# Expert token rows split once into two rounded parts, the gate moved to the scatter, six raw unit buffers

## Chip, cores and metric

One core of one Trainium2 chip runs the whole program. The metric is the device time in microseconds of one execution. A product is rounded when its operands are float32r, plain when they are float32.

## What is computed

The reference is one inference step of a two-layer decoder over 256 new tokens and 8 x 8 sampled ones, 320 tokens of width 1024. Each layer has a token mixer and a feed-forward part; in layer 0 it is dense, in layer 1 a mixture of eight experts, of which each token takes its best two:

```python
logits = x @ w_router + b_router
top_val, top_idx = lax.top_k(logits, 2)
gate = einsum(softmax(top_val), one_hot(top_idx, 8))
for e in range(8):
    out = out + gate[..., e:e + 1] * ((silu(x @ w_gate[e]) * (x @ w_up[e])) @ w_down[e])
```

with w_gate and w_up of 1024 x 2816 and w_down of 2816 x 1024 per expert. The layer's result is a layer norm of ALPHA * x + out. All of it is float32.

## The kernel before

Only the expert stage of layer 1 is touched. It works in this way.

**Tokens.** The normalised tokens x1T lie with their features on the partitions. tensor_moe (L1035) makes the router's logits on PE (L1041) and turns the tokens into rows (to_rows, L936); scalar_moe (L1370) copies these rows into xtk, three chunks of 128, 128 and 64 tokens with 1024 columns each (L1374). vector_moe (L1913) finds the chosen experts, the gates, and for each token its place in each expert's list, pos (L1970). xtk's unused 64 rows are set to zero (L1918). An expert has at most 128 places in one pass; further passes exist under a flag.

**Gather.** select(x) on DVE (L1827) makes a 0/1 matrix from pos, one column per place. gather(x) on PE (L941) multiplies the rows by it: 8 feature chunks times 3 token chunks, 24 plain products of 128 x 128 (L950). Then it turns the selection (L953), and with three products of one column makes the gate of each place (L955). ACT copies the result into a rounded tile (tokens_high, L1327) and the gate into gsl (L1329); DVE takes the difference (tokens_rest, L1842). From there on each product is three rounded ones, high x high, high x rest, rest x high (split_product, L561 to L565).

**Units.** An expert's weights come in 33 units of 1 MB. A unit is loaded by SP (unit_load, L2487, issued at L2498), copied by ACT into a rounded tile (expert_high, L1320), its difference is made by DVE (expert_rest, L1836), and PE multiplies with it: columns (L959) for gate and up, down (L979). There are MOE_RAW = 8 raw buffers: six in the tile weights and two in arena. Unit n waits, in SP's queue, until DVE has finished unit n - 8 (L2484). ACT and DVE run AHEAD = 3 units ahead of PE, over MOE_SPLIT = 4 rounded buffers. UNITS (L187) is the order in which all engines walk; tile by tile of 512 of the 2816 columns come gate units, up units and then the down units of the tile before. gather(x + 1) stands in PE's order inside expert x, behind its fourth tile (L1030).

**Gate and scatter.** gated(tile) on DVE (L1847) multiplies silu, gsl and the up product. After an expert's last down unit its output is split again (L1348, L1867), scatter on PE (L1002) multiplies it by the turned selection in six pieces of 512 columns, and add on DVE (L1870) adds each to acc, which began as ALPHA * xtk (L1883). PE's first gather waits for that scaling too (L947).

The first six units of the stage are loaded while the mixer of layer 1 still runs, each into a slot that the mixer has done with; units 6 and 7 go into arena as soon as the residual is made (L2576).

Of the kernel before, what the change touches and what calls it, by code (L numbers as in the profile page):

```python
# [6 lines left out]
P = 128  # L7
# [19 lines left out]
FF_SPLIT = 4  # L27
MOE_RAW = 8
MOE_SPLIT = 4
# [184 lines left out]
def build(nc, I, O, table):  # L214
    ctx = ExitStack()
    with ctx:
# [177 lines left out]

        xtk = view(a_kt, 3, D)
        acc = view(a_g, 3, D)

        raw = [view(i * UNIT, UNIT, of=weights) for i in FIRST_FREE] + [view(0, UNIT), view(a_o + 512, UNIT)]
        split_at = [a_u, a_u + UNIT, a_u + 2 * UNIT, a_v]
# [26 lines left out]
        gain = view(FIRST_FREE[0] * UNIT, D, of=weights)  # L426
        shift = view(FIRST_FREE[0] * UNIT + D, D, of=weights)
        selm = [room(3, P) for _ in range(2)]
        gsl = [room(1) for _ in range(2)]
        lg, expl, chosen, gate, pos = [room(3, NE) for _ in range(5)]  # L430
# [122 lines left out]
        def chunk(n):  # L553
            return slice(n * P, (n + 1) * P)
# [3 lines left out]
        def _(pe):  # L558
# [379 lines left out]

            def experts(ps):

                def gather(x):  # L941

                    pe.wait_ge(mo_sel, NE * ps + x + 1)
                    if x >= 2:
                        pe.wait_ge(mo_acc, NE * NP * ps + NP * (x - 1) + 1)
                    elif x == 0:
                        pe.wait_ge(mo_acc, NE * NP * ps + 1)  # L947
                    for k in range(KC):
                        for t in range(3):
                            nc.tensor.matmul(bank[5 + k // 4][:, chunk(k % 4)], xtk[:, t, chunk(k)],  # L950
                                             selm[x % 2][:, t, :], start=t == 0, stop=t == 2)
                    for t, (t0, r) in enumerate(TT):
                        nc.tensor.transpose(bank[7][:, t0:t0 + r], selm[x % 2][0:r, t, :], ident[0:r, 0:r])  # L953
                    for t in range(3):
                        mm = nc.tensor.matmul(bank[7][:, T:T + 1], selm[x % 2][:, t, :], gate[:, t, x:x + 1],  # L955
                                              start=t == 0, stop=t == 2)
                    mm.then_inc(mo_gath, 1)
# [77 lines left out]
            def tensor_moe(l):  # L1035
# [19 lines left out]
                pe.wait_ge(*dv_s.at("pos"))  # L1055
                pe.wait_ge(*ac_s.at("xtk"))
                experts(0)
                flag = pe.value_load(over, min_val=0, max_val=1)
# [116 lines left out]
        def _(act):  # L1175
# [146 lines left out]
            def experts(ps):  # L1322

                def tokens_high(x):
                    act.wait_ge(mo_gath, NE * ps + x + 1)
                    for i in range(2):
                        nc.scalar.activation(xgh[x % 2][:, 4 * i:4 * i + 4, :],  # L1327
                                             bank[5 + i].rearrange("p (k t) -> p k t", k=4), ACT.Copy).then_inc(mo_xh, 1)
                    nc.scalar.activation(gsl[x % 2], bank[7][:, T:T + 1], ACT.Copy)  # L1329
                    nc.scalar.activation(selT[x % 2], bank[7][:, 0:T], ACT.Copy).then_inc(mo_st, 1)  # L1330
# [39 lines left out]
            def scalar_moe(l):  # L1370
                for t, (t0, r) in enumerate(TT):
                    for i in range(2):
                        act.wait_ge(*pe_s.at("xt", l, t, i))
                        nc.scalar.activation(xtk[0:r, t, 512 * i:512 * i + 512], of(l, "xt", t, i)[0:r, :], ACT.Copy)\  # L1374
                            .then_inc(*free(ac_s, l, "xt", t, i))
                table[("act", "xtk")] = ac_s.count
                act.wait_ge(*dv_s.at("less max"))
                nc.scalar.activation(expl, expl, ACT.Exp).then_inc(*ac_s.done("exp logits"))
                act.wait_ge(*dv_s.at("pos"))
                for n, c in (("cp", 16 * HB), ("n", 32), ("conv", 32)):  # L1380
                    act.wait_ge(stored[n], c * (l + 1))
                for n in range(AHEAD):
                    expert_high(0, n)
                experts(0)
                flag = act.value_load(over, min_val=0, max_val=1)
                with act.If(flag > 0):
                    with act.Fori(1, 3) as ps:
                        for n in range(AHEAD):
                            expert_high(ps, n)
                        experts(ps)  # L1390
# [247 lines left out]
        def _(dve):  # L1638
# [186 lines left out]
            def experts(ps, first=False):  # L1825

                def select(x):  # L1827
                    if x >= 2:
                        dve.wait_ge(mo_gath, NE * ps + x - 1)
                    for t in range(3):  # L1830
                        ins = nc.vector.tensor_scalar(selm[x % 2][:, t, :], iotaF, pos[:, t, x:x + 1], None, ALU.is_equal)
                        ins.then_inc(*((mo_v, 1) if t < 2 else (mo_sel, 1)))
# [14 lines left out]
                def gated(tile):  # L1847
                    _, x, q, _, n = TILES[tile]
                    dve.wait_ge(mo_sil, NTILE * ps + tile + 1)
                    if q == 0:  # L1850
                        dve.wait_ge(mo_st, NE * ps + x + 1)
                    if tile > 0:
                        dve.wait_ge(mo_turn, NTILE * ps + tile)
                    nc.vector.scalar_tensor_tensor(hid[:, 0:n], sil[:, 0:n], gsl[x % 2], bank[1][:, 0:n], ALU.mult, ALU.mult)\
                        .then_inc(mo_h, 1)
# [14 lines left out]
                def add(x, c0, c1):  # L1870

                    dve.wait_ge(mo_acc, NE * NP * ps + NP * x + c0 + 1)
                    for p in range(c0, c1):
                        t, _, r, half = PIECES[p]
                        w = slice(512 * half, 512 * half + 512)
                        dve.wait_ge(mo_sc, NE * NP * ps + NP * x + p + 1)
                        nc.vector.tensor_tensor(acc[0:r, t, w], acc[0:r, t, w], bank[(7, 5, 6)[p % 3]][0:r, :], ALU.add)\
                            .then_inc(mo_acc, 1)

                select(0)  # L1880
                if first:
                    dve.wait_ge(*ac_s.at("xtk"))
                    nc.vector.tensor_scalar(acc, xtk, ALPHA, None, ALU.mult).then_inc(mo_acc, 1)  # L1883
                for n in range(AHEAD):
# [28 lines left out]
            def vector_moe(l):  # L1913
# [3 lines left out]
                nc.vector.memset(lg, 0.0).then_inc(*dv_s.done())  # L1917
                nc.vector.memset(xtk[NS:P, 2, :], 0.0).then_inc(*dv_s.done())  # L1918
                nc.vector.tensor_tensor(after_, causal, ident, ALU.subtract).then_inc(*dv_s.done())
# [523 lines left out]
        def _(sp):  # L2443
# [84 lines left out]
            for l in range(DEPTH):  # L2528
# [43 lines left out]
                else:  # L2572
                    for n in range(6):
                        sp.wait_ge(*pe_s.at("unit", l, *LAST_IN[FIRST_FREE[n]]))
                        unit_load(n)
                    sp.wait_ge(*dv_s.at("res1", l, KC - 1))  # L2576
                    unit_load(6)
                    unit_load(7)
                    experts(0, MOE_RAW)
# [59 lines left out]
```

## Time and profile before

| | us |
|---|---|
| median of three runs | 2387.61 (2387.57 to 2389.4) |
| the profiled execution, its own time | 2387.4 |
| its span, first to last instruction | 2385.5 |
| PE busy in the span | 2202.8 (92%) |
| DVE busy | 1578.8 (66%) |
| ACT busy | 1137.2 (48%) |
| POOL busy | 104.2 (4%) |

The span is what the trace covers; the execution's own time has 1.9 us around it. PE counts products, PEld weight loads, which overlap them; the end of a product is modelled, so the distance from one start to the next is what a product costs in a stream. A plain (f32) product leaves two loads and two products in the trace, a rounded one leaves one of each. The clock is the share of full speed granted to PE: 1.00 is 2.4 GHz, 0.50 is 1.2 GHz. Stretches named here are microseconds from the start of the span; the expert stage begins at about 1530.

### The profile page before, as it was taken

The page shows a single profiled execution, that of the slowest core. Times are in us where ns is not written, and L with a number is a line of the kernel's source. Part 1 is how long each engine was busy: PE and PEld are TensorE (multiplying, and loading weights), DVE is VectorE, ACT ScalarE, POOL GpSimd, SP SyncE. Part 2 cuts the span into 40 slices and gives each one's busy share as a digit, 9 for nine tenths or more (in the row PEclk, how much of TensorE's full clock was granted, in tenths as well). Part 3 has the DMA queues.
Part 4 walks back from the last instruction along what each step waited for, and adds up shares of the span by engine and source line. Part 5 has one row for each costly group of instructions (what it writes and reads, how often), then busy time and mean ns, then how long its engine had stood idle before and what let it go on. Part 6 is the DMA issues. An engine that isn't in the chain of part 4 may idle for free.

```text
span 2385.5 us, 31380 instructions
## 1 busy us (share of the span) xinstructions
PE 2202.8 (92%) x13148; PEld 1931.1 (81%) x13148; DVE 1578.8 (66%) x1787; ACT 1137.2 (48%) x1134; POOL 104.2 (4%) x173
## 2 busy tenths in 40 slices
PE   7889999899899988989998899799999999999996
PEld 6778767779799987878677799678888888888884
DVE  5746646656544435664745655488898988889896
ACT  4443333233333335353234232467676766767673
POOL 1001012000000000001021000000000000000000
PEclk9999999899899998999899999799999999999998
DMA  5232543654245432233525654399899999999992
GB/s 171 71 93 76 168 120 118 217 194 140 91 148 159 144 99 89 71 93 102 179 75 183 218 162 146 137 332 328 321 368 317 365 321 365 328 316 364 327 349 91
DMA packets 290491, 474.27 MB, mean 199 GB/s; under 512 B 17946, under 2 KB 160554, under 8 KB 290344
## 3 DMA queue, kind: packets, MB, share of 16 engines
q1 hardware_dynamic: 280652, 445.45, 55.3%
q0 software_dynamic: 9600, 26.75, 3.5%
q8 instruction: 106, 1.74, 0.3%
q14 instruction: 41, 0.34, 0.0%
q10 hardware_dynamic: 92, 0.00, 0.0%
HBM read 440.14 MB, written 29.92 MB: 197 GB/s over the span
## 4 chain that ended last, share of the span: by engine, by line
PE 49%; DVE 4%; ACT 2%; issue 1%; DMA 1%; SPq 0%; DVEq 0%; ACTq 0%
PE bank L563 10%; PE bank L565 10%; PE bank L564 10%; PE bank L569 3%; PE bank L571 3%; PE bank L570 3%; PE bank L950 2%; DVE mixer_rest L1682 1%; PE bank L999 1%; ACT mixer_high L1197 1%; PE bank L1014 0%; PE bank L1013 0%; PE bank L791 0%; PE bank L926 0%; PE bank L1041 0%
## 5 line engine op out<-in xcount | busy, mean ns | idle before, releaser
L1836 DVE TENSOR_TENSOR unit_rest<-weights,unit_high 128x2048 fp32r<-128x2048 f32 x198 | 452.0, 2289 | 85.8 <-ACT unit_high L1320 85.2
L1320 ACT ACTIVATE unit_high<-weights 128x2048 fp32r<-128x2048 f32 x198 | 379.3, 1919 | 158.9 <-PE bank L565 157.2
L1682 DVE TENSOR_TENSOR mixer_rest<-weights,mixer_high 128x2048 fp32r<-128x2048 f32 x86 | 196.5, 2287 | 231.1 <-ACT mixer_high L1197 231.0
L569 PE MATMUL bank<-tokens_in_high,mixer_high 128*128 128x320 f32 x896 | 295.3, 330 | 44.7 <-DVE mixer_rest L1682 37.7
L563 PE MATMUL bank<-unit_high,tokens_high 128*128 128x512 f32 (+1 forms) x768 | 291.2, 379 | 2.0 <-DVE tokens_rest L1842 2.0
L570 PE MATMUL bank<-tokens_in_rest,mixer_high 128*128 128x320 f32 x896 | 288.9, 322 | 0.0
L571 PE MATMUL bank<-tokens_in_high,mixer_rest 128*128 128x320 f32 x896 | 288.4, 322 | 0.0
L565 PE MATMUL bank<-unit_high,tokens_rest 128*128 128x512 f32 (+1 forms) x768 | 287.0, 374 | 0.0
L564 PE MATMUL bank<-unit_rest,tokens_high 128*128 128x512 f32 (+1 forms) x768 | 286.8, 373 | 0.0
L569 PEld LDWEIGHTS bank<-tokens_in_high,mixer_high 128*128 128x128 f32 x896 | 180.5, 201 | 52.1 <-DVE mixer_rest L1682 43.5
L1197 ACT ACTIVATE mixer_high<-weights 128x2048 fp32r<-128x2048 f32 x86 | 163.7, 1906 | 112.9 <-PE bank L571 58.2
L570 PEld LDWEIGHTS bank<-tokens_in_rest,mixer_high 128*128 128x128 f32 x896 | 179.7, 201 | 0.2
L571 PEld LDWEIGHTS bank<-tokens_in_high,mixer_rest 128*128 128x128 f32 x896 | 178.9, 200 | 0.0
L1836 DVE TENSOR_TENSOR unit_rest<-arena,unit_high 128x2048 fp32r<-128x2048 f32 x66 | 150.8, 2289 | 29.2 <-ACT unit_high L1320 28.9
L563 PEld LDWEIGHTS bank<-unit_high,tokens_high 128*128 128x128 f32 x768 | 145.5, 189 | 26.7 <-DVE tokens_rest L1842 2.1
L565 PEld LDWEIGHTS bank<-unit_high,tokens_rest 128*128 128x128 f32 x768 | 145.4, 189 | 26.0
L564 PEld LDWEIGHTS bank<-unit_rest,tokens_high 128*128 128x128 f32 x768 | 145.6, 190 | 24.5
L1320 ACT ACTIVATE unit_high<-arena 128x2048 fp32r<-128x2048 f32 x66 | 126.6, 1919 | 52.7 <-PE bank L565 52.7
L563 PE MATMUL bank<-unit_high,hidden_high 128*128 128x512 f32 x352 | 137.1, 390 | 1.1 <-DVE hidden_rest L1860 1.1
L565 PE MATMUL bank<-unit_high,hidden_rest 128*128 128x512 f32 x352 | 137.1, 390 | 0.0
L564 PE MATMUL bank<-unit_rest,hidden_high 128*128 128x512 f32 x352 | 137.0, 389 | 0.0
L1179 ACT ACTIVATE arena<-bank 128x320 f32<-128x320 f32 (+2 forms) x72 | 35.3, 490 | 212.6 <-PE bank L571 132.0
(417 smaller groups left out, 4317.7 us busy)
## 6 DMA issues: line engine op xcount, KB each, us to landing
weights<-in_w_ex_gate SPq DMA_DIRECT2D x67, 1024.0 KB, 6.7
weights<-in_w_in SPq DMA_DIRECT2D x66, 1024.0 KB, 5.3
weights<-in_w_ex_up SPq DMA_DIRECT2D x66, 1024.0 KB, 6.5
weights<-in_w_ex_down SPq DMA_DIRECT2D x65, 1024.0 KB, 6.8
arena<-in_w_ex_down SPq DMA_DIRECT2D x23, 1024.0 KB, 7.2
arena<-in_w_ex_up SPq DMA_DIRECT2D x22, 1024.0 KB, 7.1
arena<-in_w_ex_gate SPq DMA_DIRECT2D x21, 1024.0 KB, 7.0
weights<-in_state_mlstm_c SPq DMA_DIRECT2D x14, 1024.0 KB, 7.6
```

Source lines behind the costliest of these rows:

```text
L563: nc.tensor.matmul(out, xh, wh, start=start, stop=False)
L564: nc.tensor.matmul(out, xh, wl, start=False, stop=False)
L565: return nc.tensor.matmul(out, xl, wh, start=False, stop=stop)
L569: nc.tensor.matmul(out, wh, xh, start=start, stop=False)
L570: nc.tensor.matmul(out, wh, xl, start=False, stop=False)
L571: return nc.tensor.matmul(out, wl, xh, start=False, stop=stop)
L950: nc.tensor.matmul(bank[5 + k // 4][:, chunk(k % 4)], xtk[:, t, chunk(k)], selm[x % 2][:, t, :], start=t == 0, stop=t == 2)
L1179: nc.scalar.activation(dst, of(l, name, i, m)[0:rows, 0:cols], ACT.Copy)\
L1197: nc.scalar.activation(split_at_home(l, *u)[0], place_, ACT.Copy).then_inc(*ac_s.done("unit high", l, *u))
L1320: nc.scalar.activation(high[n % MOE_SPLIT], raw[n % MOE_RAW], ACT.Copy).then_inc(mo_high, 1)
L1682: nc.vector.tensor_tensor(wl, unit_at(l, *u)[0], wh, ALU.subtract).then_inc(*dv_s.done("unit rest", l, *u))
L1836: nc.vector.tensor_tensor(rest[n % MOE_SPLIT], raw[n % MOE_RAW], high[n % MOE_SPLIT], ALU.subtract)\
```

## The change

The token rows are no longer kept as they are and gathered by plain products. ACT copies the rows from PSUM into acc, then copies acc into a rounded tile xth; DVE subtracts xth from acc into three rounded tiles xtl, and only then scales acc by ALPHA. The selection is written as a rounded tile. gather multiplies first xth, then xtl, for each feature chunk and token chunk: 48 rounded products where 24 plain ones stood; the third chunk is used with its 64 rows alone, so nothing has to be set to zero. The first gather waits for xtl and no longer for the scaled acc.

The products that gathered the gate, ACT's copy of it and DVE's wait for that copy are gone. gated multiplies silu and up only; add multiplies each scattered piece by the token's gate while it adds it.

xtl takes the places of the two raw buffers in arena. So there are six, SP waits for unit n - 6, and the two loads behind the residual are gone.

```diff
@@ -25,7 +25,7 @@
 FF_SPLIT = 4
-MOE_RAW = 8
+MOE_RAW = 6
 MOE_SPLIT = 4
@@ -392,10 +392,11 @@
 
-        xtk = view(a_kt, 3, D)
+        xth = rounded("token_rows_high", a_kt, 3, D)
+        xtl = [rounded(f"token_rows_rest{t}", at, D) for t, at in enumerate((0, D, a_o + 512))]
         acc = view(a_g, 3, D)
 
-        raw = [view(i * UNIT, UNIT, of=weights) for i in FIRST_FREE] + [view(0, UNIT), view(a_o + 512, UNIT)]
+        raw = [view(i * UNIT, UNIT, of=weights) for i in FIRST_FREE]
         split_at = [a_u, a_u + UNIT, a_u + 2 * UNIT, a_v]
@@ -425,8 +426,9 @@
         shift = view(FIRST_FREE[0] * UNIT + D, D, of=weights)
+        room((-at[0]) % 8)
+        selr = [rounded(f"selection{i}", at[0] + 3 * P * i, 3, P) for i in range(2)]
         selm = [room(3, P) for _ in range(2)]
-        gsl = [room(1) for _ in range(2)]
         lg, expl, chosen, gate, pos = [room(3, NE) for _ in range(5)]
@@ -936,24 +938,23 @@
 
-            def experts(ps):
+            def experts(ps, first=False):
 
...
                         pe.wait_ge(mo_acc, NE * NP * ps + NP * (x - 1) + 1)
-                    elif x == 0:
+                    elif x == 0 and not first:
                         pe.wait_ge(mo_acc, NE * NP * ps + 1)
                     for k in range(KC):
-                        for t in range(3):
-                            nc.tensor.matmul(bank[5 + k // 4][:, chunk(k % 4)], xtk[:, t, chunk(k)],
-                                             selm[x % 2][:, t, :], start=t == 0, stop=t == 2)
+                        out = bank[5 + k // 4][:, chunk(k % 4)]
+                        for t, (_, r) in enumerate(TT):
+                            for i, rows in enumerate((xth[0:r, t, :], xtl[t][0:r, :])):
+                                nc.tensor.matmul(out, rows[:, chunk(k)], selr[x % 2][0:r, t, :],
+                                                 start=t + i == 0, stop=t + i == 3)
                     for t, (t0, r) in enumerate(TT):
-                        nc.tensor.transpose(bank[7][:, t0:t0 + r], selm[x % 2][0:r, t, :], ident[0:r, 0:r])
-                    for t in range(3):
-                        mm = nc.tensor.matmul(bank[7][:, T:T + 1], selm[x % 2][:, t, :], gate[:, t, x:x + 1],
-                                              start=t == 0, stop=t == 2)
+                        mm = nc.tensor.transpose(bank[7][:, t0:t0 + r], selm[x % 2][0:r, t, :], ident[0:r, 0:r])
                     mm.then_inc(mo_gath, 1)
@@ -1053,8 +1054,8 @@
                 pe.wait_ge(*dv_s.at("pos"))
-                pe.wait_ge(*ac_s.at("xtk"))
-                experts(0)
+                pe.wait_ge(*dv_s.at("xtl"))
+                experts(0, True)
                 flag = pe.value_load(over, min_val=0, max_val=1)
@@ -1326,7 +1327,6 @@
                                              bank[5 + i].rearrange("p (k t) -> p k t", k=4), ACT.Copy).then_inc(mo_xh, 1)
-                    nc.scalar.activation(gsl[x % 2], bank[7][:, T:T + 1], ACT.Copy)
                     nc.scalar.activation(selT[x % 2], bank[7][:, 0:T], ACT.Copy).then_inc(mo_st, 1)
@@ -1371,11 +1371,14 @@
                         act.wait_ge(*pe_s.at("xt", l, t, i))
-                        nc.scalar.activation(xtk[0:r, t, 512 * i:512 * i + 512], of(l, "xt", t, i)[0:r, :], ACT.Copy)\
+                        nc.scalar.activation(acc[0:r, t, 512 * i:512 * i + 512], of(l, "xt", t, i)[0:r, :], ACT.Copy)\
                             .then_inc(*free(ac_s, l, "xt", t, i))
...
                 nc.scalar.activation(expl, expl, ACT.Exp).then_inc(*ac_s.done("exp logits"))
+                act.wait_ge(*ac_s.at("xtk"))
+                nc.scalar.activation(xth[:, 0:2, :], acc[:, 0:2, :], ACT.Copy)
+                nc.scalar.activation(xth[0:NS, 2, :], acc[0:NS, 2, :], ACT.Copy).then_inc(*ac_s.done("xth"))
                 act.wait_ge(*dv_s.at("pos"))
@@ -1828,7 +1831,7 @@
                     for t in range(3):
-                        ins = nc.vector.tensor_scalar(selm[x % 2][:, t, :], iotaF, pos[:, t, x:x + 1], None, ALU.is_equal)
+                        ins = nc.vector.tensor_scalar(selr[x % 2][:, t, :], iotaF, pos[:, t, x:x + 1], None, ALU.is_equal)
                         ins.then_inc(*((mo_v, 1) if t < 2 else (mo_sel, 1)))
@@ -1847,11 +1850,9 @@
                     dve.wait_ge(mo_sil, NTILE * ps + tile + 1)
-                    if q == 0:
-                        dve.wait_ge(mo_st, NE * ps + x + 1)
                     if tile > 0:
                         dve.wait_ge(mo_turn, NTILE * ps + tile)
-                    nc.vector.scalar_tensor_tensor(hid[:, 0:n], sil[:, 0:n], gsl[x % 2], bank[1][:, 0:n], ALU.mult, ALU.mult)\
+                    nc.vector.tensor_tensor(hid[:, 0:n], sil[:, 0:n], bank[1][:, 0:n], ALU.mult)\
                         .then_inc(mo_h, 1)
@@ -1874,13 +1875,21 @@
                         dve.wait_ge(mo_sc, NE * NP * ps + NP * x + p + 1)
-                        nc.vector.tensor_tensor(acc[0:r, t, w], acc[0:r, t, w], bank[(7, 5, 6)[p % 3]][0:r, :], ALU.add)\
+                        nc.vector.scalar_tensor_tensor(acc[0:r, t, w], bank[(7, 5, 6)[p % 3]][0:r, :], gate[0:r, t, x:x + 1],
+                                                       acc[0:r, t, w], ALU.mult, ALU.add)\
                             .then_inc(mo_acc, 1)
...
                 if first:
-                    dve.wait_ge(*ac_s.at("xtk"))
-                    nc.vector.tensor_scalar(acc, xtk, ALPHA, None, ALU.mult).then_inc(mo_acc, 1)
+                    dve.wait_ge(*ac_s.at("xth"))
+                    for t, (_, r) in enumerate(TT):
+                        nc.vector.tensor_tensor(xtl[t][0:r, :], acc[0:r, t, :], xth[0:r, t, :], ALU.subtract)\
+                            .then_inc(*dv_s.done())
+                    table[("dve", "xtl")] = dv_s.count
+                    settle()
+                    nc.vector.tensor_scalar(acc[:, 0:2, :], acc[:, 0:2, :], ALPHA, None, ALU.mult).then_inc(*dv_s.done())
+                    nc.vector.tensor_scalar(acc[0:NS, 2, :], acc[0:NS, 2, :], ALPHA, None, ALU.mult).then_inc(mo_acc, 1)
+                    settle()
                 for n in range(AHEAD):
@@ -1915,7 +1924,6 @@
                 nc.vector.memset(lg, 0.0).then_inc(*dv_s.done())
-                nc.vector.memset(xtk[NS:P, 2, :], 0.0).then_inc(*dv_s.done())
                 nc.vector.tensor_tensor(after_, causal, ident, ALU.subtract).then_inc(*dv_s.done())
@@ -2573,9 +2581,6 @@
                         unit_load(n)
-                    sp.wait_ge(*dv_s.at("res1", l, KC - 1))
-                    unit_load(6)
-                    unit_load(7)
                     experts(0, MOE_RAW)
```

## Rows read from the trace of the kernel before

**Rows 1.** Page part 4: the chain that ended last, by engine

```profile
PE 49%; DVE 4%; ACT 2%; issue 1%; DMA 1%; SPq 0%; DVEq 0%; ACTq 0%
```

**Rows 2.** Busy us gather to gather: PE, PEld, DVE, ACT, POOL; clock, DMA share

```profile
1610.68:1712.92 102.24, 102.24 (x513) 86.17 (x512) 88.06 (x59) 70.71 (x52) 0.00 (x0) 1.00 0.95 341
...
sum 715.62, PE 715.62 PEld 603.11 DVE 616.12 ACT 494.90 POOL 0.00; mean PE 102.23 PEld 86.16 DVE 88.02 ACT 70.70 POOL 0.00
```

**Rows 3.** Timeline of PE at the second gather: start us, us, instruction

```profile
1610.68 5.52 PE L950 MATMUL bank<-arena 128*128 128x128 f32 x48
1616.04 0.58 PE L953 MATMUL bank<-arena 128*128 128x128 f32 x3
1616.56 0.83 PE L955 MATMUL bank<-arena 128*128 128x1 f32 x6
1617.25 0.48 PE L563 MATMUL bank<-unit_high,tokens_high 128*128 128x512 f32 x1
```

**Rows 4.** The chain that ended last, at the first gather: start, us, what

```profile
1527.88 0.23 ACT arena L1378
...
1529.71 0.68 DVE arena L1831 x3
1530.39 1.68 DVE arena L1883
...
1532.20 7.23 PE bank L950 x48
...
1540.65 0.61 ACT tokens_high L1327
...
1547.27 1.92 ACT unit_high L1320
```

**Rows 5.** Weight loads by form near 1615 and 1683: busy us, mean ns

```profile
L950 PEld LDWEIGHTS bank<-arena 128*128 128x128 f32 x48 | 5.4, 192 | 0.0
...
L1013 PEld LDWEIGHTS bank<-outputs_high,selection_turned 128*128 128x128 f32 x4 | 0.8, 188 | 0.2
...
L1013 PEld LDWEIGHTS bank<-outputs_high,selection_turned 128*64 128x64 f32 x2 | 0.3, 134 | 0.1
```

**Rows 6.** Timeline of PE in 256-wide rounded products

```profile
1636.85 0.28 PE L565 MATMUL bank<-unit_high,tokens_rest 128*128 128x256 f32 x1
...
1637.92 0.28 PE L565 MATMUL bank<-unit_high,tokens_rest 128*128 128x256 f32 x1
```

**Rows 7.** Groups of ACT and DVE with 1024 columns: busy us, mean ns

```profile
L1296 ACT ACTIVATE dense_high<-weights 128x1024 fp32r<-128x1024 f32 x2 | 2.1, 1062 | 10.3 <-PE bank L571 10.3
...
L1794 DVE TENSOR_TENSOR dense_rest<-weights,dense_high 128x1024 fp32r<-128x1024 f32 x2 | 2.5, 1226 | 6.2 <-ACT dense_high L1296 6.2
```

**Rows 8.** Busy us by stretch, columns as above, around the first gather

```profile
1512.10:1519.00 6.90, 6.90 (x33) 6.88 (x33) 1.42 (x4) 0.00 (x0) 0.00 (x0) 0.50 0.00 0
1528.90:1535.60 6.70, 3.40 (x16) 3.43 (x17) 6.60 (x13) 5.51 (x3) 0.00 (x0) 0.50 0.03 2
...
1559.60:1562.90 3.30, 3.30 (x9) 2.55 (x8) 1.35 (x2) 0.00 (x0) 0.00 (x0) 0.50 1.01 390
```

**Rows 9.** Waits of SP's queue from 1480 on: us in total, times, longest

```profile
SPq L2498 <- DVE unit_rest L1836: 733.6, 256, 38.1
```

**Rows 10.** Landings of all unit loads (L2498)

```profile
DMA to landing us min/median/max: 4.9/6.7/9.2
```

**Rows 11.** Timeline of SP and ACT for one unit and the load two on

```profile
1658.37 0.37 SPq L2498 DMA_DIRECT2D arena<-in_w_ex_up  x1
...
1663.81 0.37 SPq L2498 DMA_DIRECT2D weights<-in_w_ex_down  x1
...
1676.26 1.92 ACT L1320 ACTIVATE unit_high<-arena 128x2048 fp32r<-128x2048 f32 x1 [0.80 <-PE bank L565]
```

**Rows 12.** Groups of DVE by form, 1640 to 1720: busy us, mean ns

```profile
L1854 DVE SCALAR_TENSOR_TENSOR arena<-arena,bank 128x512 f32<-128x512 f32 x4 | 2.9, 737 | 0.0
...
L1877 DVE TENSOR_TENSOR arena<-arena,bank 128x512 f32<-128x512 f32 x4 | 2.5, 678 | 0.0
```

## Prediction

> **What bounds the kernel now.** I began at the page: PE holds 49% of the chain that ended last, all else that it names 8% together [rows 1]. The change touches only the expert stage, so I cut that stage into experts, from the start of one gather to the start of the next. All seven such stretches are alike: 102.2 us, PE busy in every one of them, DVE for 88 us, ACT for 71 us, the clock at 1.00 [rows 2]. Whatever PE no longer does there comes straight off the time, until another engine has no air: DVE has 14 us of it per expert. Then I read what PE does between two experts' units [rows 3]: the gather (24 f32 products, each recorded as two loads and two products, 48 records in 5.36 us from 1610.68 to 1616.04), three turns (0.52 us), and three products with the gate column (6 records, 0.69 us from 1616.56 to 1617.25). Last I read the chain at the first gather, the one place where PE waits on a string of other engines [rows 4].
>
> **The gate products go.** They end each gather, so 0.69 us of PE goes from seven stretches: 7 x 0.69 = **4.8 us less**. The first gather's share is in the sum of the start, below. ACT also loses its copy of the gate column; ACT has 31 us of air per expert, so that is worth nothing.
>
> **The gather, 24 f32 products against 48 rounded ones.** The name "single-pass" suggests half the work. But each of the 48 takes a fresh 128 x 128 weight load, and the old code has 48 loads as well. The gate products stream one column each and still took 0.69 / 6 = 115 ns, against 5.36 / 48 = 112 ns for a record that streams 128 columns twice [rows 3]. So at full clock the load sets the pace, not the stream. Is a rounded operand's load any shorter? No: 188 ns for the rounded 128 columns of L1013 and 134 for 64, beside 192 for the f32 ones of L950 [rows 5]; the difference of 54 ns per 64 columns makes about 107 ns of loading per 128. No rounded product as narrow as 128 columns is in the trace. From below: the 256-wide rounded products start 119 ns apart (nine steps from 1636.85 to 1637.92 [rows 6]), and if columns alone counted, 128 would take 59 ns, 2.9 us per gather. From above, as rounded products: those same 119 ns, 5.7 us. I take 112 ns, the row with the same load, the same width and the same neighbours: 48 x 112 ns = 5.4 us, **no change**; the two ends per gather are -2.5 and +0.35 us. The third chunk's products on 64 rows I cost as full ones.
>
> The Trainium skill ("TensorE: Matmul & The Clock Gate", Back-to-back issue gap) gives about 81 ns for a load and product pair of 128 columns, and its section on weight-path perf modes lets the fast weight load work for types other than FP32. By that the gather would be an estimated 3.9 us; the rows show the rounded load as long as the f32 one, which speaks against it.
>
> **The start of the expert stage.** Before: selection on DVE from 1529.71, then the scaling of all token rows until 1532.07, then PE [rows 4]. After: ACT, free at 1528.1, copies the rows into a rounded tile, 1.9 us for two chunks of 1024 columns (as the unit copy at 1547.27, 2048 columns [rows 4]) and 1.06 for the third [rows 7], until 1531.1. DVE, done with selecting at 1530.4, waits 0.7 us for it and makes three differences of 1024 columns, 1.2 us each [rows 7], until 1534.7. The scaling, now in two pieces of together some 1.8 us (L1883 took 1.7 [rows 4]), stands behind them and no longer ahead of the gather. So the gather starts at about 1534.85, **2.65 us later**. What stands behind the new work: ACT's first three unit copies start at 1531.1 and not 1529.71; DVE's first two unit differences end at 1534.7 + 1.9 + 4.5 = 1541.1. Both are hidden as long as the gather lasts to 1545; if it were 3.5 us long they would show.
>
> The clock there is at 0.50 from 1528.90 to 1535.60 [rows 8], since PE had nothing to do. In the old gather, two full streams per load followed and the clock came back after 16 records of 213 ns; the whole took 7.23 us [rows 4]. The logits' f32 products, which stream 8 columns behind each load, ran 6.9 us without a break, 209 ns each, and the clock stayed at 0.50 throughout [rows 8]: loads without much streaming did not bring it back. The new gather streams half of what the old one did per load, so I expect it at the lower level to its end: 48 x 213 ns = 10.2 us, three turns 0.6, and 0.25 to ACT: 1545.9, where ACT's copy began at 1540.65 [rows 4]: **5.25 us later**. The first unit's products then start in the slow clock too; 0.35 us more. Together **+5.6 us** (ends +2.6, if the clock comes back as before, and +6.5). The missing wait of the first gather for the scaled rows is in this sum.
>
> **Six raw buffers.** A load is issued when DVE has finished the unit that held the slot: all 256 waited for that, 734 us in total [rows 9], so the queue always stands ready. Loads land 9.2 us after issue at the latest, 6.7 in the middle [rows 10]. One unit in full: issued 1658.37, read by ACT at 1676.26, 17.9 us later. With six slots it goes out when the load two units on did, at 1663.81: 12.5 us before its reader [rows 11]. The longest landing leaves 3.3 us. **Zero**; if landings became 4 us longer, each further microsecond would be PE's per unit. At the start units 6 and 7 are no longer loaded ahead; they follow the first two differences (1538.9, 1541.1), land by 1550.3; ACT copied unit 4 at 1547.27 [rows 4], two units of 1.9 us before it could take unit 6, and all of that moves 5.6 us back. Hidden.
>
> **Vector forms.** The hidden rows lose a scalar operand (737 ns towards the 678 of a plain one), the scattered rows gain one (678 to about 737) [rows 12]: within 0.5 us per expert on DVE, hidden by its 14. Behind the last scatter two such adds are in the open: **+0.1**. The dropped memset ran while DVE waited for the logits: zero.
>
> **Sum.** -4.8 + 0 + 5.6 + 0 + 0.1 = +0.9 us on the profiled execution's 2387.4 (span 2385.5 and 1.9 around it): 2388.3; the median of the runs is 0.2 above that execution, so 2388.5. A measurement here can tell about 0.2%, 4.8 us, from no change: this forecast is no change.
>
> **Rivals.**
> 1. *The clock falls inside the later gathers* (slower). Place: the 5.4 us gather of each expert, where the stream per load is half of the old one. For it: the clock did sit at 0.50 through 6.9 us of load-bound products [rows 8]. Against it: that stretch streamed 8 columns, this one 128, and it comes straight out of dense products at 1.00. Price: a stretch at 0.50 (1.2 GHz) ran nine 512-wide products in 3.30 us [rows 8] where 2.4 GHz does it in half the time: 1.65 us lost per such stretch, twice that if the thin gather keeps it down. It decides from the point where most of the gathers fall: 7 x 1.65 = 11.6, time **2400** (2393 for a few, 2406 if they stay down). Chance 0.33.
> 2. *The rounded load does not bind* (faster). By the lower bound 59 ns: seven gathers save 2.5 each, 17.5; the first gather at half clock is about 5.1 us, so the start costs nothing: 2387.6 - 4.8 - 17.5 = **2365**. The Trainium skill's 81 ns (page and section above) would make it an estimated 2378. Against it are [rows 3, 5]. Chance 0.11.
> 3. *The change doesn't do what it says*: a narrow rounded product runs as slowly as the f32 one it replaces. 24 took 5.36 us, 48 would take 10.7: 7 x 5.36 = 37.5 more, less 4.8, and at the start 2.65 and 48 more records at 112 ns, less the gate's 0.7, some 7: **2428**. The rounded products in the trace are all 256 wide or wider, so no row excludes it. Chance 0.07.
> 4. *A late unit*: the 3.3 us of margin are gone; a microsecond on some units per expert, about 2395. Chance 0.03.
>
> **Numbers.** My forecast has 0.46; it lies between 2385 (the clock comes back in the first gather) and 2392 (119 ns per product). The range also takes in most of rival 1 and rival 4: 2385 to 2404; left out are rivals 2, 3 and the top of 1, 0.2. Faster by over 0.2%: rival 2, 0.11. Within: 0.46. Slower: rivals 1, 3 and 4, 0.43.
>
> **What would show it.** Right: 48 gather records some 112 ns apart, as before, and stretches of 101.5 us; the first gather near 10 us with its first product 2 to 3 us later; no DMA as releaser of an ACT copy. Rival 1 shows in the granted clock of the windows at each gather, rival 2 and 3 in the spacing of the gather's records. A first gather of 7 us or less, or ACT waiting for landings, would prove my steps wrong.

## The result and the profile after

The changed kernel takes **2431.48 us** (2430.61 to 2437.86), the kernel before 2387.65 us beside it: ratio 1.0188, interval 1.0169 to 1.0206. It is slower, and above the predicted range of 2385 to 2404. The profiled execution has a span of 2430.4 us, 44.9 more than before, and a mean clock of 0.944 against 0.958.

The page, part 4 (the chain that ended last, by line; PE's gather is L954 now), to be set against [rows 1]:

```profile
PE bank L571 11%; PE bank L565 11%; PE bank L566 11%; PE bank L567 11%; PE bank L573 11%; PE bank L572 11%; PE bank L954 3%; ACT mixer_high L1198 2%; DVE mixer_rest L1685 2%; PE bank L660 2%; PE bank L928 1%; PE bank L793 1%; SPq L2558 1%; PE bank L1000 1%; DVE arena L1744 1%
```

The gather, L954, stands in it with 3%; L950 had 2% before. The stretches from one gather to the next (columns as in [rows 2]: length, PE, PEld, DVE, ACT, POOL, clock, DMA share, GB/s), two of six and their sum:

```profile
1725.75:1834.15 108.40, 108.40 (x509) 89.99 (x507) 88.13 (x59) 70.66 (x51) 0.00 (x0) 0.95 0.90 320
1834.15:1940.93 106.78, 106.78 (x508) 88.75 (x507) 88.03 (x59) 70.74 (x51) 0.00 (x0) 0.97 0.90 325
...
sum 645.57, PE 645.57 PEld 536.23 DVE 529.01 ACT 424.30 POOL 0.00; mean PE 107.59 PEld 89.37 DVE 88.17 ACT 70.72 POOL 0.00
```

PE is still busy all the time, but the stretches are 106.8 and 108.4 us long, not 102.2, and the clock is no longer 1.00. It goes to 0.50 once in each of the seven later gathers, each time until after the gather's end. Windows laid on those times, two of seven and their sum:

```profile
1731.11:1741.35 10.24, 10.24 (x31) 8.04 (x31) 0.00 (x0) 0.00 (x0) 0.00 (x0) 0.50 0.38 150
1840.33:1847.16 6.83, 6.83 (x21) 5.23 (x21) 0.00 (x0) 0.00 (x0) 0.00 (x0) 0.50 0.44 174
...
sum 58.04, PE 58.04 PEld 45.14 DVE 0.00 ACT 0.00 POOL 0.00; mean PE 8.29 PEld 6.45 DVE 0.00 ACT 0.00 POOL 0.00
```

The first gather, in the chain that ended last (to be set against [rows 4]):

```profile
1528.80 0.22 ACT arena L1378
1529.02 1.80 ACT token_rows_high L1380
1530.82 0.96 ACT token_rows_high L1381
...
1531.80 3.50 DVE token_rows_rest L1886 x3
...
1535.38 13.32 PE bank L954 x48
1548.71 0.93 PE bank L957 x3
...
1549.65 0.61 ACT tokens_high L1328
...
1551.63 0.80 PE bank L565
```

The start is as the prediction's steps have it: ACT rounds, DVE subtracts, then PE. But the 48 products take 13.32 us, not 10.2. Where the 44.9 us of span lie:

| | before | after | more |
|---|---|---|---|
| first gather starts at | 1532.20 | 1535.38 | 3.2 |
| from there to the second gather | 78.48 | 83.53 | 5.1 |
| six stretches, gather to gather | 613.4 | 645.57 | 32.2 |
| last gather's start to the end of the span | 161.5 | 165.9 | 4.4 |

Of the 3.2 us, 0.9 is older than the change: ACT's L1378 ends that much later in this execution already.

What a later gather looks like inside stands in the timeline of PE, one feature chunk at full clock, products first:

```profile
1726.96 0.28 PE L954 MATMUL bank<-selection,token_rows_high 128*128 128x128 f32 x1
1727.08 0.27 PE L954 MATMUL bank<-selection,token_rows_rest 128*128 128x128 f32 x1
1727.28 0.32 PE L954 MATMUL bank<-selection,token_rows_high 64*128 64x128 f32 x1
1727.44 0.27 PE L954 MATMUL bank<-selection,token_rows_rest 64*128 64x128 f32 x1
1727.65 0.33 PE L954 MATMUL bank<-selection,token_rows_high 128*128 128x128 f32 x1
1727.81 0.28 PE L954 MATMUL bank<-selection,token_rows_rest 128*128 128x128 f32 x1
1727.92 0.27 PE L954 MATMUL bank<-selection,token_rows_high 128*128 128x128 f32 x1
```

and the weight loads of the same products:

```profile
1727.02 0.19 PEld L954 LDWEIGHTS bank<-selection,token_rows_rest 128*128 128x128 f32 x1
1727.28 0.18 PEld L954 LDWEIGHTS bank<-selection,token_rows_high 64*128 64x128 f32 x1
1727.39 0.19 PEld L954 LDWEIGHTS bank<-selection,token_rows_rest 64*128 64x128 f32 x1
1727.64 0.19 PEld L954 LDWEIGHTS bank<-selection,token_rows_high 128*128 128x128 f32 x1
1727.75 0.19 PEld L954 LDWEIGHTS bank<-selection,token_rows_rest 128*128 128x128 f32 x1
```

Loads with the same row count start 110 ns apart. Where the row count goes from 128 to 64 or back, the next load starts 250 to 260 ns after the last, together with its own product and no longer ahead of it. The product at the change comes 0.20 us after its neighbour and the one behind it 0.16, where 0.11 each is the rule: 0.14 us per change, two changes per chunk, 16 per gather, 2.3 us.

### The profile page after: what moved, and what is told of

It reads as the page before. It is cut to its first block, busy times and chain, and to the rows that moved or that the text cites. A ratio compares the mean times of both kernels' runs of the same rounds, so it can differ in the third digit from the quotient of the medians.

```text
span 2430.4 us, 31274 instructions
## 1 busy us (share of the span) xinstructions
PE 2245.3 (92%) x13100; PEld 1956.6 (81%) x13100; DVE 1582.1 (65%) x1790; ACT 1139.9 (47%) x1128; POOL 104.2 (4%) x173
## 4 chain that ended last, share of the span: by engine, by line
PE 80%; DVE 10%; ACT 6%; issue 2%; DMA 1%; SPq 1%; POOL 0%; DVEq 0%; ACTq 0%; POOLq 0%
PE bank L571 11%; PE bank L565 11%; PE bank L566 11%; PE bank L567 11%; PE bank L573 11%; PE bank L572 11%; PE bank L954 3%; ACT mixer_high L1198 2%; DVE mixer_rest L1685 2%; PE bank L660 2%; PE bank L928 1%; PE bank L793 1%; SPq L2558 1%; PE bank L1000 1%; DVE arena L1744 1%
## 5 line engine op out<-in xcount | busy, mean ns | idle before, releaser
L1839 DVE TENSOR_TENSOR unit_rest<-weights,unit_high 128x2048 fp32r<-128x2048 f32 x264 | 602.5, 2289 | 150.7 <-ACT unit_high L1321 148.9
L1321 ACT ACTIVATE unit_high<-weights 128x2048 fp32r<-128x2048 f32 x264 | 505.9, 1919 | 246.3 <-PE bank L567 246.3
L565 PE MATMUL bank<-unit_high,tokens_high 128*128 128x512 f32 (+1 forms) x768 | 297.3, 387 | 2.0 <-DVE tokens_rest L1845 2.0
L566 PE MATMUL bank<-unit_rest,tokens_high 128*128 128x512 f32 (+1 forms) x768 | 291.8, 380 | 0.0
L1797 DVE TENSOR_TENSOR dense_rest<-weights,dense_high 128x2048 fp32r<-128x2048 f32 (+1 forms) x34 | 75.6, 2229 | 62.4 <-ACT dense_high L1297 62.4
L571 PE MATMUL bank<-dense_x_high,dense_high 128*128 128x320 f32 x352 | 109.8, 312 | 6.7 <-DVE dense_x_rest L1804 6.6
```

What stands on the lines that cost most here:

```text
L565: nc.tensor.matmul(out, xh, wh, start=start, stop=False)
L566: nc.tensor.matmul(out, xh, wl, start=False, stop=False)
L571: nc.tensor.matmul(out, wh, xh, start=start, stop=False)
L1321: nc.scalar.activation(high[n % MOE_SPLIT], raw[n % MOE_RAW], ACT.Copy).then_inc(mo_high, 1)
L1797: nc.vector.tensor_tensor(ff_rest[u % FF_RAW][:, 0:n], ff_raw[u % FF_RAW][:, 0:n], ff_high[u % FF_SPLIT][:, 0:n], ALU.subtract).then_inc(f ...
L1839: nc.vector.tensor_tensor(rest[n % MOE_SPLIT], raw[n % MOE_RAW], high[n % MOE_SPLIT], ALU.subtract)\
```

## The experiments

The theory from this profile: the gather's products on 128 rows cost what was forecast; the loss is in the changes of row count, directly and through the clock. Eleven kernels, all timed beside the kernel before. "Row changes" are those from one product of a later gather to the next, 128 rows to 64 or back, with the one from its last product to the turns; the third turn's own two, in every kernel, are left out. "Falls" are later gathers (of seven) in or right behind which the clock went to 0.50; the gather's length is that at full clock.

| kernel | later gather | row changes | us | falls | stretch, us | time, us | ratio (interval) |
|---|---|---|---|---|---|---|---|
| before | 24 plain | 0 | 5.4 | 0 | 102.2 | | 1 |
| after | 48 rounded | 16 | 7.7 | 7 | 106.8, 108.4 | 2431.5 | 1.0188 (1.0169 to 1.0206) |
| e1_full_rows | 48 rounded | 0 | 5.4 | 0 | 101.6 | 2389.2 | 0.9998 (0.9988 to 1.0008) |
| e2_grouped | 48 rounded | 4 | 5.9 | 4 | 102.2 to 105.2 | 2404.4 | 1.0074 (1.0057 to 1.0090) |
| e3_gate_only | 24 plain | 0 | 5.4 | 0 | 101.6 | 2381.6 | 0.9974 (0.9963 to 0.9984) |
| e4_plain_64_rows | 24 plain | 16 | 8.4 | 0 | 105.3 | 2416.8 | 1.0121 (1.0104 to 1.0138) |
| e5_six_raw | 24 plain | 0 | 5.4 | 0 | 102.2 | 2388.4 | 0.9998 (0.9989 to 1.0007) |
| e6_gate_free_start | 24 plain | 0 | 5.4 | 0 | 101.6 | 2381.6 | 0.9968 (0.9957 to 0.9979) |
| e7_stacked | 40 rounded | 0 | 4.5 | 0 | 100.7 | 2380.6 | 0.9969 (0.9957 to 0.9981) |
| e8_late_split | 40 rounded | 0 | 4.5 | 0 | 100.7 | 2375.3 | 0.9944 (0.9930 to 0.9957) |
| e9_fill | 56 rounded | 16 | 8.9 | 7 | 109.6 to 111.2 | 2449.6 | 1.0264 (1.0247 to 1.0282) |
| e10_twice | 96 rounded | 0 | 10.7 | 0 | 106.9 | 2425.4 | 1.0159 (1.0143 to 1.0176) |
| e11_high_alone | 24 rounded | 16 | 5.0 | 7 | 102.7 to 104.2 | 2405.7 | 1.0078 (1.0061 to 1.0095) |

**Full rows.** The changed kernel with the third chunk filled up with zeros:

```diff
-for t, (_, r) in enumerate(TT):
-    for i, rows in enumerate((xth[0:r, t, :], xtl[t][0:r, :])):
-        nc.tensor.matmul(out, rows[:, chunk(k)], selr[x % 2][0:r, t, :],
+for t in range(3):
+    for i, rows in enumerate((xth[:, t, :], xtl[t])):
+        nc.tensor.matmul(out, rows[:, chunk(k)], selr[x % 2][:, t, :],
...
```

What is cut from it here sets acc's empty 64 rows to zero and splits all 128.

> The changed kernel, with the third token chunk gathered on all 128 rows (zeros in the empty 64) instead of 64. Theory: two things made the gather dear. Going from 128 rows to 64 and back between products costs some 0.14 us each time, 16 times per gather, 2.3 us; and the clock falls to 0.50 because so few columns stream per load. With full rows the first must go: 48 records 112 ns apart at full clock. If the second needs the first (the gaps of the switches thin the stream), the clock stays at 1.00 in the later gathers, stretches are 101.6 us and the time is about 2389. Rival: thin rounded products lower the clock by themselves; then there are still stretches at 0.50 at the gathers and the time is 2410 to 2420.

One later stretch, and all later gathers together:

```profile
1721.09:1822.69 101.60, 101.60 (x509) 85.47 (x507) 88.24 (x59) 70.70 (x51) 0.00 (x0) 1.00 0.95 342
...
1619.49:2360.00 740.51, 739.66 (x3688) 622.60 (x3686) 639.35 (x417) 512.32 (x363) 0.00 (x0) 1.00 0.94 336
```

With the same products on 128 rows the stretch is 0.6 us shorter than before, the clock stays, and the time is that of the forecast. So the third chunk's 64 rows, where 128 would do, are what costs 42 us (2431.5 against 2389.2).

**Grouped.** The changed kernel, per bank first the 16 products on 128 rows, then the 8 on 64:

```diff
+for b in range(2):
+    for some in ((0, 1), (2,)):
+        for c in range(4):
+            for t in some:
...
```

> The changed kernel, its 48 products in another order: per bank first the 16 on 128 rows, then the 8 on 64 rows, so that rows change 3 times per gather and not 15. If each change of rows costs 0.14 us, a gather at full clock falls from 7.7 to about 5.9 us; if the 64-row products themselves are dear (164 ns each), it stays near 6.4. Clock kept: 2392. Clock still falling: 2412 to 2422.

A stretch without a fall and one with:

```profile
1718.22:1820.37 102.15, 102.15 (x508) 85.73 (x507) 88.14 (x59) 70.65 (x51) 0.00 (x0) 1.00 0.94 339
1922.52:2027.74 105.22, 105.22 (x508) 87.99 (x507) 88.22 (x59) 70.71 (x51) 0.00 (x0) 0.97 0.92 329
```

Four changes cost 102.15 - 101.60 = 0.55 us, 0.14 each, as in the timeline: the direct cost goes with their number, and not with that of the 64-row products (the gather takes 5.9 us, not 6.4). The fall costs another 3.07 us for 6.83 us at 0.50, so 0.45 us for each microsecond at the lower level. The time lies between the two that were expected, since the clock fell in four gathers of seven.

**Gate alone.** The kernel before, with the gate applied in add:

```diff
...
-for t in range(3):
-    mm = nc.tensor.matmul(bank[7][:, T:T + 1], selm[x % 2][:, t, :], gate[:, t, x:x + 1], ...
...
-nc.vector.tensor_tensor(acc[0:r, t, w], acc[0:r, t, w], bank[(7, 5, 6)[p % 3]][0:r, :], ALU.add)
+nc.vector.scalar_tensor_tensor(acc[0:r, t, w], bank[(7, 5, 6)[p % 3]][0:r, :], gate[0:r, t, x:x + 1], ...
```

> The kernel before with the gate moved to the scatter and nothing else: plain gather, eight raw buffers. Theory: the gate part of the change was right, 0.69 us off seven stretches and off the first gather: 2382 (ratio 0.9977). Rival: the scaled adds or the missing wait cost something: 2387 or more.

```profile
1709.53:1811.16 101.63, 101.63 (x508) 85.49 (x506) 88.22 (x59) 70.70 (x51) 0.00 (x0) 1.00 0.95 341
```

0.6 us per stretch, and 7.0 us between the medians. This part of the change is a gain by itself.

**Plain, 64 rows.** The kernel before, its third chunk used with 64 rows:

```diff
-for t in range(3):
-    nc.tensor.matmul(..., xtk[:, t, chunk(k)], selm[x % 2][:, t, :], start=t == 0, stop=t == 2)
+for t, (_, r) in enumerate(TT):
+    nc.tensor.matmul(..., xtk[0:r, t, chunk(k)], selm[x % 2][0:r, t, :], start=t == 0, stop=t == 2)
```

> The kernel before, its plain gather using the third chunk with 64 rows, nothing else. If the change of rows costs by itself, the plain records show the same pattern (two longer distances after each change, about 2.3 us per gather) at a clock of 1.00, and the time is 2406. If the cost is one of rounded products alone, it is 2387 to 2389.

```profile
1724.46:1829.77 105.31, 105.31 (x514) 87.30 (x513) 88.09 (x59) 70.71 (x52) 0.00 (x0) 1.00 0.92 329
...
1619.16:2390.00 770.84, 768.51 (x3741) 637.43 (x3739) 639.15 (x418) 513.24 (x372) 0.00 (x0) 1.00 0.89 320
```

So the cost is not one of rounded products: among plain ones each change is dearer, (105.31 - 102.24) / 16 = 0.19 us. But here the clock holds in the later gathers, through the same 16 changes. The rest of its 28 us, and most of what it took beyond the 2406 expected, is the first stretch, 86.4 us where before it was 78.5: the clock, at 0.50 when that gather begins, stays there until 1556.7.

**Six raw buffers alone**, on the kernel before:

```diff
-MOE_RAW = 8
+MOE_RAW = 6
...
-raw = [...] + [view(0, UNIT), view(a_o + 512, UNIT)]
+raw = [...]
...
-sp.wait_ge(*dv_s.at("res1", l, KC - 1))
-unit_load(6)
-unit_load(7)
```

> The kernel before with nothing but six raw unit buffers in place of eight: the two buffers in the arena go, and with them the wait and the two early loads. Theory (units land far ahead of ScalarE, so the buffers cost nothing): the time of before, 2387 to 2390 us, and no ScalarE wait for a load in the expert stage. Rival (a unit comes late at the start of the stage, as priced in the prediction's fourth rival): 2392 to 2395 us with an idle stretch of ScalarE released by a load.

What ACT waited for in the expert stage (total us, times, longest):

```profile
ACT unit_high L1320 <- PE bank L565: 209.1, 197, 7.7
...
ACT unit_high L1320 <- DVE arena L1970: 1.6, 1, 1.6
```

No wait for a load; the time is that of before. In the changed kernel, too, ACT's unit copies waited for PE alone (246.3 us, 197 times). The step stands.

**Twice, and the high part alone.** Two ways to tell the changes of row count from the mere length of a thin, rounded gather. One makes the products of the full-row kernel's later gathers twice (its edit is shown against that kernel), the other leaves the rest rows' products out of the changed kernel's:

```diff
-for k in range(KC):
+for k in [*range(KC), *(range(KC) if x > 0 else ())]:
```
```diff
-for i, rows in enumerate((xth[0:r, t, :], xtl[t][0:r, :])):
+for i, rows in enumerate((xth[0:r, t, :], xtl[t][0:r, :])[:1 if x > 0 else 2]):
...
```

> The full-row kernel (48 products of 128 rows per gather, no change of row count, 2389.2 us) with each later gather's products made twice, the second round overwriting the first with the same values: 96 products of 112 ns, 10.8 us. Theory R (the changes of row count bring the clock down in the later gathers): no fall, later stretches of 107.0 us, 2427 us. Rival L (what counts is that the thin rounded gather lasts longer than the old 5.4 us; the changes of row count only made it longer): the clock falls in each later gather, stretches of 110 to 112 us, 2448 to 2460 us.

> The changed kernel with the products of the rest rows left out of the later gathers (the expert inputs then lack that part): 24 rounded products, still 16 changes of row count, as a product of 64 rows stands between two of 128 in each chunk; a chunk of some 0.57 to 0.62 us, a gather of 4.6 to 5.0 us. Theory R (the changes of row count bring the clock down): a fall in most later gathers, stretches of 104 us and more, 2407 to 2417 us. Rival L (the length of the thin gather does): no fall, stretches near 101 us, about 2385 us.

The first kernel, a stretch and all later gathers:

```profile
1722.12:1829.04 106.92, 106.92 (x557) 90.84 (x555) 88.24 (x59) 70.73 (x51) 0.00 (x0) 1.00 0.89 325
...
1615.17:2395.00 779.83, 778.72 (x4032) 661.59 (x4030) 639.58 (x417) 512.38 (x363) 0.00 (x0) 1.00 0.88 319
```

and the second, one gather and what followed it:

```profile
1824.63:1829.36 4.73, 4.73 (x27) 3.66 (x25) 4.31 (x3) 2.32 (x2) 0.00 (x0) 1.00 1.10 359
1829.36:1836.18 6.82, 6.82 (x18) 5.09 (x18) 0.10 (x1) 0.00 (x0) 0.00 (x0) 0.50 0.65 257
```

A gather of 10.7 us without a change of row count keeps the clock at 1.00; one of 5.0 us with 16 of them has 0.50 in it or right behind it, seven times of seven (its 2405.7 us are 1.3 under the time expected for that). The length is not the cause; among rounded products the falls come with the changes of row count.

**Filled.** More streaming in the changed gather:

```diff
 out = bank[5 + k // 4][:, chunk(k % 4)]
+if x > 0:
+    nc.tensor.matmul(bank[5 + k // 4][:, P * (k % 4):512], xth[:, 0, chunk(k)],
+                     xgh[(x - 1) % 2][:, k % 4:4, :].rearrange("p k t -> p (k t)"), start=True, stop=True)
```

> The changed kernel, changes of row count and all, with one more rounded product of 512 to 128 columns ahead of each feature chunk of the later gathers (8 per gather, on operands at hand, into columns that the chunk's own products then overwrite). Theory (the clock falls in the later gathers because PE streams so little there, the changes of row count being the larger part of it): with the added streaming the clock stays at 1.00 in all later gathers; a chunk takes 0.96 us and about 0.15 more, a gather 8.9 us, a later stretch about 105 us against 106.8 and 108.4 of the changed kernel, and the time is about 2414 us, less than the changed kernel's 2431.5 us in spite of 56 more products. Rival (the clock falls with the changes of row count or with rounded narrow products, whatever stands between them): a fall in each gather, stretches of 108 to 110 us, 2440 to 2450 us.

```profile
1735.12:1745.36 10.24, 10.24 (x34) 8.31 (x34) 0.00 (x0) 0.00 (x0) 0.00 (x0) 0.50 0.36 144
...
1953.57:1967.23 13.66, 13.66 (x44) 11.05 (x43) 0.00 (x0) 0.07 (x1) 0.00 (x0) 0.50 0.32 128
```

A miss for the theory that the clock falls because PE streams too little there: it fell in every later gather all the same, and the time came out at the rival's end. But the theory is not refuted by that. The eight products add 2560 columns to 48 x 128, and the gather takes 8.9 us at full clock where the full-row one takes 5.4, so it still streams less per microsecond than the full-row one. In each kernel whose clock fell, the changes also made the stream thinner than that. Whether they act by themselves or through the thinner stream, and why plain products hold the clock, is not settled.

**A start without the scaling.** The gate-only kernel, its first gather not waiting for the scaled rows:

```diff
-elif x == 0:
+elif x == 0 and not first:
     pe.wait_ge(mo_acc, NE * NP * ps + 1)
```

> The gate moved to the scatter, as in the gate-only kernel (2381.6 us), and the first gather no longer waits until VectorE has scaled the accumulator (1.68 us on that kernel's chain). Theory (that scaling alone ends last there): 2379.9 us, first product of the gather 1.7 us earlier. Rival (what follows, the first units' rounding on ScalarE or the first rest on VectorE, takes the wait over): 2381 to 2382 us.

Its chain:

```profile
1530.51 8.03 PE bank L950 x48
...
1553.27 2.29 DVE unit_rest L1832
```

No gain: 2381.6 us both. The gather starts at 1530.51, not 1531.77, but the clock is at 0.50 until 1535.2 there and 1535.6 here, so more of it runs slowly: 8.03 us, not 7.23. Its second unit's difference is still ahead, at 1553.27 where the gate-only kernel has it at 1554.09. Then the clock is at 0.50 once more, from 1556.09 to 1559.50, as it is not in the gate-only kernel there, and the second gather starts later (1608.65, not 1607.90). One profile of each doesn't show whether the earlier start causes that.

**Stacked.** The changed kernel, the third chunk's 64 rest rows laid under its 64 rounded ones in one operand:

```diff
...
+for i, (t, rows) in enumerate(((0, xth[:, 0, :]), (0, xtl[0]), (1, xth[:, 1, :]), (1, xtl[1]), (2, xth[:, 2, :]))):
+    nc.tensor.matmul(out, rows[:, chunk(k)], selr[x % 2][:, t, :], start=i == 0, stop=i == 4)
...
+nc.vector.tensor_tensor(xtl[t] if t < 2 else xth[NS:P, 2, :], acc[0:r, t, :], xth[0:r, t, :], ALU.subtract)
...
+nc.vector.scalar_tensor_tensor(pos[NS:P, 2, :], rk[0:NS, 2 * NE:3 * NE], 1.0, chosen[0:NS, 2, :], ...
```

> The changed kernel with the third chunk's 64 rounded rows and 64 rest rows laid under one another in one operand of 128 rows, and the positions doubled to match: 40 products of 128 rows in a gather, no change of row count. Theory (each product costs its load, 112 ns at full clock and 213 ns at half, and a change of row count is what the 64-row products cost): against the full-row kernel (2389.2 us) 8 products less per gather, 7 x 0.90 + 1.7 = 8.0 us less: 2381.2 us, later stretches of 100.7 us, the clock at 1.00 in all of them. Rival (the clock falls in the later gathers as soon as the products are rounded and narrow): 2402 to 2415 us. Rival (not the load but something else sets the pace of the gather): no gain against 2389 us.

```profile
1716.54:1817.24 100.70, 100.70 (x501) 84.58 (x499) 88.14 (x59) 70.66 (x51) 0.00 (x0) 1.00 0.96 344
```

Eight products fewer, 101.60 - 100.70 = 0.90 us: 112 ns each, the load's price.

**Late split.** Stacked, but with a plain first gather, and the split and the scaling done piece by piece in the first expert:

```diff
+if first and x == 0:
+    for t in range(3):
+        nc.tensor.matmul(out, acc[:, t, chunk(k)], selm[0][:, t, :], start=t == 0, stop=t == 2)
+    continue
...
```

> As the stacked kernel, but the first gather runs on the plain rows (24 products as in the kernel before, straight from the copied rows, not waiting for the split or the scaling), and the rounding, the subtraction and the scaling are done later in the first expert, between its units. Theory (the late start and the low clock of the first gather are the rest of what the split costs): the first gather starts some 5 us earlier and lasts 7.2 instead of 8.5 us: 2374.5 us, from 2381.2 us, and below the gate-only kernel's 2381.6 us. Rival (the 2.8 us of ScalarE and the 5.3 us of VectorE that move into the first expert delay its units): 2377 to 2382 us.

The chain at the first gather of the stacked kernel, then of this one:

```profile
1535.60 8.77 PE bank L954 x40
```
```profile
1531.69 7.92 PE bank L956 x48
```

The gather begins 3.9 us sooner and is 0.85 us shorter; 5.3 us come off between the medians. At 2375.3 us this is the fastest kernel here, ahead of the one before (0.9944) and of the changed one.

## Why the prediction was wrong

**The gather (forecast: no change).** The step that failed is its last sentence, "The third chunk's products on 64 rows I cost as full ones". All else in it held: the load sets the pace, a rounded load of 128 columns is as long as a plain one, and 48 products of 128 rows take what 48 records took (full rows; stacked). But there are 16 changes of row count in each gather, at 0.14 us each where the clock is full: 2.3 us, times seven. The profile of before had shown such a change, in a row that the prediction reads: the three turns took 0.52 us [rows 3], not three times 112 ns, and the third of them is on 64 rows. The weight loads there:

```profile
1615.94 0.25 PEld L953 LDWEIGHTS bank<-arena 128*128 128x128 f32 x2
1616.35 0.13 PEld L953 LDWEIGHTS bank<-arena 64*128 64x128 f32 x1 [0.17 <-issue]
1616.56 0.74 PEld L955 LDWEIGHTS bank<-arena 128*128 128x128 f32 x6
```

PEld stands still for 0.17 us ahead of the load on 64 rows, and the next one, on 128 rows again, starts 0.21 us behind it, where 0.11 is the rule. The turns' excess of 0.18 us makes 0.09 us for each of the two changes; by that price 16 would have been an estimated 1.5 us per gather, not nothing.

The Trainium skill ("TensorEngine Tiling (Array Packing)", Key Properties) has the rule that was overlooked: changing the tiling mode "drains the TensorE". The trace agrees, if 64 rows count as such a mode: the load at a change no longer starts ahead of its product.

**Rival 1.** It came true, and dearer: its place (the later gathers) and sign were right, its price of 1.65 us was for the shorter of the falls seen. They last 6.83 or 10.24 us, 3.1 or 4.6 us lost, in sum 58.04 x 0.45 = 26 us. Its reason was not enough: 128 columns behind each load, with no change of row count, did not bring the clock down (full rows; twice). With the changes among rounded products it fell; whether they do it by themselves or through the thinner stream that they leave is open.

**Rivals 2 to 4** did not happen. The Trainium skill's 81 ns per pair ("TensorE: Matmul & The Clock Gate", Back-to-back issue gap) is not borne out: a pair takes 112 ns here (full rows; stacked).

**The start (+5.6 us).** The first product was forecast 2.65 us later; it is 2.3, once the 0.9 us from earlier is taken off. The clock stays at 0.50 through the gather, as forecast. The gather's 10.2 us are right for full rows, 13.3 with the changes, which at half clock cost 0.19 us each (345 + 274 ns instead of twice 213): 16 x 0.19 = 3.1. The same failed term again.

**The gate (-4.8)**: 0.6 us per stretch, 7.0 us in all by the medians with an interval of some 2.5 us to either side; right within that. **Six raw buffers (0)**: right. **Vector forms**: DVE has 88.2 us per stretch in the mean, against 88.0 before; the 0.1 us behind the last scatter is too little to be seen.

**The sum.** Without the failed term the forecast was 2388.5 us, and the kernel without it takes 2389.2. Part of that closeness is luck: the interval leaves some 2.4 us to either side, and in that kernel's profile the second gather starts 3.8 us later than before, not 5.6, once the 5.0 us by which ACT's L1378 already ended later are taken off. What came on top: 26 us of clock in the later gathers, about 16 of changes there, and 3 in the first, 45 by these prices; the two kernels' distances from the one before differ by 43.

## What to carry to other kernels

Before a chunk is cut to its true rows, look at what stands next to it in PE's order: a product on 64 rows between products on 128 saves no time where the load sets the pace, and costs two changes of row count. Fill it up, put the odd chunks side by side, or best stack two half operands into one full one, which also drops a product. Where the profile has a product on fewer rows anywhere, read what stands before and behind it. And take a change with several parts apart: here one part gained 7 us, one did nothing, and one detail of the third lost 42.

## What was not expected of the hardware

- A change of row count in a stream of products costs 0.14 us (rounded) and 0.19 us (plain) at 2.4 GHz, 0.19 us (rounded) at 1.2 GHz; the next load is not taken ahead.
- Behind or within rounded gathers with 16 such changes the clock went to 0.50 every time (21 of 21 gathers in three kernels), with 4 changes in 4 of 7, with none never, be the gather 4.5 or 10.7 us long. Plain products with 16 changes never did in a later gather. What makes the difference is open; eight more products of 128 to 512 columns per gather did not cure it.
- One microsecond at the lower level cost 0.45 us of time (grouped: 3.07 us for 6.83), though most of it fell into the dense products behind the gather.
